# A four-layer decoder step: DVE takes part of the convolution's taps, and attention's queries are split and used ahead of the keys

## What is computed

```python
def conv_module(h, ctx, w_pw1, b_pw1, w_dw, b_dw, ln_g, ln_b, w_pw2, b_pw2):
    a = h @ w_pw1 + b_pw1
    a = a[..., :D_MODEL] * jax.nn.sigmoid(a[..., D_MODEL:])
    full = jnp.concatenate([ctx, a], 1)
    y = lax.conv_general_dilated(full, w_dw[:, None, :], window_strides=(1,), padding='VALID',
                                 dimension_numbers=('NWC', 'WIO', 'NWC'),
                                 feature_group_count=D_MODEL) + b_dw
    y = jax.nn.silu(layer_norm(y, ln_g, ln_b))
    return y @ w_pw2 + b_pw2, full[:, -(CONV_WIDTH - 1):]

def mla_project(h, pos, w_down, g_q, g_kv, w_uq, w_uk):
    ...
    d = h @ w_down
    q_lat = rms_norm(d[..., :MLA_Q_RANK], g_q)                                      # 384
    ckv = rms_norm(d[..., MLA_Q_RANK:MLA_Q_RANK + MLA_KV_RANK], g_kv)               # 256
    kr = rope(d[..., MLA_Q_RANK + MLA_KV_RANK:][:, :, None, :], pos)[:, :, 0]       # 64
    q = (q_lat @ w_uq).reshape(bsz, t, MLA_HEADS, MLA_NOPE + MLA_ROPE)
    ...
```

## Time and profile before

| | us |
|---|---|
| median of 3 runs | 3004.7 |
| lowest and highest | 3002.46, 3007.76 |
| the profiled execution | 3006.55 |
| its span | 3004.8 |
| PE busy in the span | 2908.9 (97%) |
| DVE, POOL, ACT busy | 1643.8 (55%), 1699.8 (57%), 926.0 (31%) |
| convolution, first tap matmul to first statistics product | 864.3 to 989.5 |
| attention, first query transpose to first rope product | 1540.0 to 1553.8 |

### The profile page before, as it was taken

How to read it: one execution, slowest core, us unless ns; L and a number is a source line. 1 busy time by engine, 2 the same in 40 slices (tenths; PEclk the granted TensorE clock), 3 DMA queues, 4 the chain that set the end, 5 groups by cost and what they waited for, 6 DMA issues and landing times.

```text
span 3004.8 us, 53453 instructions
## 1 busy us (share of the span) xinstructions
PE 2908.9 (97%) x21220; PEld 2681.8 (89%) x21220; DVE 1643.8 (55%) x3121; ACT 926.0 (31%) x1813; POOL 1699.8 (57%) x1177
## 2 busy tenths in 40 slices
PE   5999999999999999999989999999999999999997
PEld 4789999999976799999976689999997999999997
DVE  3153684636563784636565548463663536856363
ACT  2220142414230352414233315241423301425141
POOL 2546546868655445857620044685764465468685
PEclk8999999999999999999999999999999999999999
DMA  6643434333344434444321334444422333222332
GB/s 229 249 112 92 124 116 162 99 113 112 100 121 134 170 116 160 151 136 148 97 64 44 95 124 136 148 146 141 140 79 85 96 91 103 67 82 85 88 96 74
DMA packets 450485, 354.84 MB, mean 118 GB/s; under 512 B 26120, under 2 KB 424832, under 8 KB 437933
## 3 DMA queue, kind: packets, MB, share of 16 engines
q1 hardware_dynamic: 435744, 324.79, 35.1%
q10 hardware_dynamic: 14493, 26.63, 3.0%
HBM read 337.86 MB, written 5.25 MB: 114 GB/s over the span
## 4 chain that ended last, share of the span: by engine, by line
PE 81%; DVE 7%; issue 3%; ACT 3%; POOL 2%; DVEq 1%; DMA 1%; POOLq 1%; ACTq 1%; SPq 1%
PE pb L1153 79%; POOL w_lo L1004 1%; DMA ada_first<-in_ada_w 1%; DVE part L2778 1%; ACT h_hi L2145 1%; POOLq L1003 1%; ACT hf L2145 1%; DVE pb L2797 1%; PE pb L1989 1%; DVE xa L2804 0%; DVE h_lo L2828 0%; DVE pr L3107 0%; PE pb L1266 0%; DVE part L2773 0%; ACTq L2442 0%
## 5 line engine op out<-in xcount | busy, mean ns | idle before, releaser
L1001 POOL TENSOR_SCALAR w_hi<-w_raw 128x1024 fp32r<-128x1024 f32 (+2 forms) x272 | 295.9, 1088 | 751.0 <-DMA w_raw<-in_gmlp_w_in 275.7
L1004 POOL TENSOR_TENSOR w_lo<-w_raw,w_hi 128x1024 fp32r<-128x1024 f32 (+2 forms) x272 | 653.1, 2401 | 45.0 <-issue 45.0
L1153 PE MATMUL pb<-a_hi,w_hi 128*128 128x288 f32 x2176 | 593.8, 297 | 2.1 <-DVEq L3392 1.9
L1153 PE MATMUL pb<-a_lo,w_hi 128*128 128x288 f32 x2176 | 588.4, 294 | 0.0
L1153 PE MATMUL pb<-h_hi,w_hi 128*128 128x288 f32 x2144 | 563.9, 299 | 18.0 <-DVE pr L3084 7.9
L1153 PE MATMUL pb<-h_lo,w_hi 128*128 128x288 f32 x2144 | 545.6, 296 | 0.0
L1046 POOL TENSOR_TENSOR w_lo<-w_raw,w_hi 128x512 fp32r<-128x512 f32 x288 | 382.3, 1349 | 180.0 <-DVE s_raw L3049 83.2
L1153 PEld LDWEIGHTS pb<-h_hi,w_hi 128*128 128x128 f32 x2144 | 392.8, 188 | 33.4 <-DVE pr L3084 10.9
L1153 PEld LDWEIGHTS pb<-a_hi,w_hi 128*128 128x128 f32 x2176 | 408.3, 188 | 8.8 <-POOL a_lo L1071 4.2
L1153 PEld LDWEIGHTS pb<-a_lo,w_hi 128*128 128x128 f32 x2176 | 408.6, 188 | 0.8
L1153 PEld LDWEIGHTS pb<-h_lo,w_hi 128*128 128x128 f32 x2144 | 389.5, 189 | 0.0
(11 more groups left out here) (379 smaller groups left out, 4875.9 us busy)
## 6 DMA issues: line engine op xcount, KB each, us to landing
ada_w<-in_ada_w SPq DMA_DIRECT2D x80, 1024.0 KB, 7.7
w_raw<-in_ffn_w_gate SPq DMA_DIRECT2D x88, 512.0 KB, 3.8
w_raw<-in_ffn_w_up SPq DMA_DIRECT2D x88, 512.0 KB, 3.8
w_raw<-in_gmlp_w_in SPq DMA_DIRECT2D x64, 512.0 KB, 4.2
w_raw<-in_ffn_w_down SPq DMA_DIRECT2D x64, 512.0 KB, 4.3
w_raw<-in_gmlp_w_out SPq DMA_DIRECT2D x32, 512.0 KB, 4.7
w_raw<-in_ffn_w_down SPq DMA_DIRECT2D x32, 384.0 KB, 3.9
w_raw<-in_conv_w_pw SPq DMA_DIRECT2D x24, 512.0 KB, 3.9
```

The lines of the kernel that those rows point to most:

```text
L1001: nc.gpsimd.tensor_scalar(w_hi[:, s, 0:w], w_raw[:, s, 0:w], 1.0, 1.0, ALU.mult, ALU.mult).then_inc(split_hi, 1)
L1004: nc.gpsimd.tensor_tensor(w_lo[:, s, 0:w], w_raw[:, s, 0:w], w_hi[:, s, 0:w].bitcast(F32), ALU.subtract).then_inc(split_lo, 1)
L1153: return nc.tensor.matmul(out, lhsT, rhs, start=start, stop=stop)
```

## The change

**Convolution.** `PE_TAPS` gives the groups of taps that stay on PE for each tile: 6, 5, 5, 5, 5, 6, 8, 8. POOL builds only these diagonals. DVE adds the missing 7 (tiles 0 and 5) or 11 taps (tiles 1 to 4) itself, one SCALAR_TENSOR_TENSOR of 512 columns each, from `full` into the bank that PE filled, with a drain behind each, before it takes the bank out. In `taps` the sums of tile m-1 now stand between the two halves of the gate of tile m+2; the rows_ready drain and `complete` follow the second half.

**Attention.** ACT makes the queries' upper parts (`query_upper`), DVE only the lower ones (`query_lower`), as each pair of banks is turned. The queries come first on DVE; scaling and rotating the keys (`scale_keys`, `turn_keys`) and the evacuation of the rope products (`query_rows`) alternate. On PE the rope products stand ahead of the key transposes, which go to the auxiliary banks; ACT copies them after issuing the four output transfers.

```diff
+PE_TAPS = (6, 5, 5, 5, 5, 6, TG, TG)
...
                     last = nc.gpsimd.tensor_tensor(
-                        diag[:, m % 2, q], mask4[:].unsqueeze(1).to_broadcast([P, TG, QC]),
-                        w4[:, q, m, :].unsqueeze(2).to_broadcast([P, TG, QC]), ALU.mult)
+                        diag[:, m % 2, q, 0:PE_TAPS[m]], mask4[:].unsqueeze(1).to_broadcast([P, PE_TAPS[m], QC]),
+                        w4[:, q, m, 0:PE_TAPS[m]].unsqueeze(2).to_broadcast([P, PE_TAPS[m], QC]), ALU.mult)
...
-                    for g in range(TG):
+                    for g in range(PE_TAPS[m]):
                         for q in range(QT):
                             last = mm(out[QC * q:QC * (q + 1), 0:c1 - c0], diag[:, m % 2, q, g, :],
-                                      x4[:, m % 2, q, QT * g + c0:QT * g + c1], g == 0, g == TG - 1)
+                                      x4[:, m % 2, q, QT * g + c0:QT * g + c1], g == 0, g == PE_TAPS[m] - 1)
...
                     if m < KT - 2:
-                        for h in range(2):
-                            gated_in(m + 2, h, h)
-                        dve.drain().then_inc(rows_ready, 1)
-                        complete(m + 2)
+                        gated_in(m + 2, 0, 0)
                     if m:
                         dve.wait_ge(ysq_ready, m)
...
                         last_.then_inc(q_done, 1)
+                    if m < KT - 2:
+                        gated_in(m + 2, 1, 1)
+                        dve.drain().then_inc(rows_ready, 1)
+                        complete(m + 2)
                     sample_taps(m)
-                    v.tensor_scalar(one(yc, m, slice(0, SEQ)), pb[:, aux(), :], one1(par, m, C_DW), None, ALU.add
+                    sums_ = pb[:, aux(), :]
+                    for w in range(QT * PE_TAPS[m], CW):
+                        v.scalar_tensor_tensor(out=sums_, in0=full[:, m % 3, w:w + SEQ], scalar=wdT[:, m, w:w + 1],
+                                               in1=sums_, op0=ALU.mult, op1=ALU.add)
+                        dve.drain()
+                    v.tensor_scalar(one(yc, m, slice(0, SEQ)), sums_, one1(par, m, C_DW), None, ALU.add
                                     ).then_inc(aux_free, 1)
...
+                def query_upper(k):
+
+                    b_p, b_s = [BANKS + (ql_at[0] + 2 * k + i) % BANKS for i in range(2)]
+                    act.wait_ge(ql_turned, 2 * k + 2)
+                    fn(ql_hi[:, k, 0:SEQ], pb[:, b_p, :], ACT.Copy)
+                    fn(ql_hi[:, k, SEQ:], pb[:, b_s, NS:P], ACT.Copy).then_inc(ql_upper, 1)
+
+                for k in range(2):
+                    query_upper(k)
                 square_sums(1, KVR, QR, range(4, TT))
...
+                query_upper(2)
                 act.wait_ge(kv_ready, 1)
...
+                def query_lower(k):
+
+                    dve.wait_ge(ql_upper, k + 1)
+                    for cols, src in ((slice(0, SEQ), slice(0, SEQ)), (slice(SEQ, TOK), slice(NS, P))):
+                        v.tensor_tensor(ql_lo[:, k, cols], pb[:, aux_of(X.n), src], ql_hi[:, k, cols].bitcast(F32),
+                                        ALU.subtract).then_inc(aux_free, 1)
+                        X.up()
...
+                for k in range(3):
+                    query_lower(k)
+                dve.drain().then_inc(lat_ready, 1)
+                scale_keys(2, 0, 4)
+                for n in range(2):
+                    query_rows(n)
+                turn_keys(0, 4)
+                for n in range(2, 5):
+                    query_rows(n)
+                scale_keys(3, 4, TT)
+                turn_keys(4, TT)
                 dve.sem_inc(kv_ready, 1)
-                evac_latents((1, 2))
-                dve.drain().then_inc(lat_ready, 1)
...
+                for n in range(5, 10):
+                    query_rows(n)
+                X.up(BANKS)
```

More of the change, by code:

```diff
@@ L447, in trunk @@
         kt_ready = sem("kt_ready")
-        kt_copied = sem("kt_copied")
+        ql_turned = sem("ql_turned")
+        ql_upper = sem("ql_upper")
         ql_scaled = sem("ql_scaled")
@@ L757, in trunk @@
         turn_at = []
+        ql_at, keys_at = [], []
         stat_banks = {}
@@ L1857, in mla @@
                 pe.wait_ge(ql_scaled, 1)
+                ql_at.append(X.n)
                 for k in range(3):
[L1859 to L1870, removed]
+                    for tts in (range(4), (4,)):
+                        b = aux_bank()
+                        for tt in tts:
+                            last = nc.tensor.transpose(pb[:, b, tt % 4 * P:(tt % 4 + 1) * P],
+                                                       dtok[:, tt, k * P:(k + 1) * P], ident[:])
+                        last.then_inc(ql_turned, 1)
+                        X.up()
                 pe.wait_ge(lat_ready, 1)
@@ L1876, in mla @@
                                   (lambda k: ql_hi[:, k, token_tile(tt)], lambda k: ql_lo[:, k, token_tile(tt)]))
+                pe.wait_ge(kv_ready, 1)
+                pe.wait_ge(aux_free, X.n + BANKS)
+                keys_at.append(X.n)
+                banks = [BANKS + (X.n + i) % BANKS for i in range(BANKS)]
+                for k in range(3):
+                    for tt in range(TT):
+                        rows = (ckv[:, tt, k * P:(k + 1) * P] if k < 2
+                                else kr2[:, tt, :, :].rearrange("p a n -> p (a n)"))
+                        out = pb[:, banks[k], tt * P:(tt + 1) * P] if tt < 4 else pb[:, banks[3], k * P:(k + 1) * P]
+                        last = nc.tensor.transpose(out, rows, ident[:])
+                    last.then_inc(kt_ready, 1)
+                X.up(BANKS)
                 def absorb(h):
@@ L1905, in mla @@
                         absorb(h - 1)
+                    else:
+                        pe.wait_ge(aux_free, X.n + BANKS)
                     expand(aux_bank(), lambda c: ukr[:, c, h * P:(h + 1) * P], lambda c: ckvT[:, c, 0:SEQ])
@@ L2517, in mla @@
                 square_sums(1, KVR, QR, range(4))
-                square_sums(1, KVR, QR, range(4, TT))
[L2519 to L2524, removed]
+                def query_upper(k):
[5 more added lines that the diff above has]
+                    query_upper(k)
+                square_sums(1, KVR, QR, range(4, TT))
+                query_upper(2)
                 act.wait_ge(kv_ready, 1)
@@ L2532, in mla @@
                               ).then_inc(kv_out, 16)
+                key_banks = [BANKS + (keys_at[0] + i) % BANKS for i in range(BANKS)]
+                for k in range(3):
+                    act.wait_ge(kt_ready, k + 1)
+                    fn(ckvT[:, k, 0:SEQ] if k < 2 else krT[:, 0:SEQ], pb[:, key_banks[k], :], ACT.Copy
+                       ).then_inc(aux_free, 1)
+                ps = pb[:, key_banks[3], :]
+                fn(ckvT[:, :, SEQ:], ps[:, 0:2 * P].rearrange("p (k t) -> p k t", k=2)[:, :, NS:], ACT.Copy)
+                fn(krT[:, SEQ:], ps[:, 2 * P + NS:3 * P], ACT.Copy)
+                act.drain().then_inc(aux_free, 1)
                 G.up(10 + 3 * HEADS)
@@ L3456, in scale_queries, with scale_keys @@
                     last_.then_inc(ql_scaled, 1)
-                def latents(n, t0, t1):
+                def scale_keys(n, t0, t1):
                     dve.wait_ge(ssq_ready, n)
@@ L3466, in latents, with turn_keys @@
                                                scalar=ssq[:, tt, 1:2], in1=gqk[:, QR:], op0=ALU.mult, op1=ALU.mult)
+                def turn_keys(t0, t1):
                     cos, sin = rtab[:, t0:t1, 0:half], rtab[:, t0:t1, half:]
@@ L3482, in latents, with query_rows @@
                     dve.drain()
[L3484 to L3487, removed]
+                def query_lower(k):
[3 more added lines that the diff above has]
+                                        ALU.subtract).then_inc(aux_free, 1)
+                        X.up()
+                def query_rows(n):
+                    c, tt = divmod(n, TT)
+                    dve.wait_ge(acc_ready, G.n + 1)
+                    v.tensor_copy(qrt[:, tt, c * 256:(c + 1) * 256], pb[:, G.n % BANKS, 0:256]).then_inc(acc_free, 1)
+                    G.up()
                 for i, (c, tt) in enumerate(first_order(len(DCH))):
@@ L3501, in mla @@
                             scale_queries()
[L3502 to L3505, removed]
-                dve.sem_inc(kv_ready, 1)
-                evac_latents((1, 2))
-                dve.drain().then_inc(lat_ready, 1)
[L3509 to L3514, removed]
+                for k in range(3):
+                    query_lower(k)
[8 more added lines that the diff above has]
+                turn_keys(4, TT)
+                dve.sem_inc(kv_ready, 1)
+                for n in range(5, 10):
+                    query_rows(n)
+                X.up(BANKS)
                 def rotate(tt):
```

## The result

| | before | changed |
|---|---|---|
| median, us (7 runs each, side by side) | 3003.5 | 3015.46 |
| lowest and highest | 3002.34, 3007.76 | 3012.16, 3017.68 |
| ratio | | 1.0037, 95% interval 1.0026 to 1.0049 |
| profiled execution and its span | 3006.55, 3004.8 | 3016.51, 3014.4 |
| statistics of the convolution: first matmul over `yc` starts | 989.48 | 1010.49 |

The account below looks back on a forecast made before the run. PE bounds the kernel before; in the changed convolution DVE, delayed by POOL, was expected to cost more than PE saves. Convolution +14.8 and attention -5.5 gave +9.3 us on 3004.7, so 3014.0 us, range 2992 to 3021.

Parts of the forecast that it names:

- PE's saving, 12.4 us: Convolution: 16 tap groups leave PE, 14.2 us; tile 0's two count nothing, leaving 12.4 us if PE stays the bound.
- The adds, 0.84 us each: Convolution: DVE's 58 added taps take 0.84 us each with drain, 48.7 us together, not held up by POOL.
- Ordinary meetings, 19.4 us: Convolution: DVE instructions wholly in SBUF wait out POOL's where prod_used doesn't set it up; 19.4 us over tiles 0 to 6.
- Built-in meetings, three of four: Convolution, tiles 2 to 5: prod_used releases POOL's 4.1 us product, DVE's bias add waits it out; three times, 12.3 us.
- b: Convolution: DVE's total delay beside POOL, 31.7 us (ends 19.4 and 36); the convolution changes by b - 16.9 us.
- PE waits: Convolution: sign that PE waits on DVE's gate before the products of tiles 5, 6 and 7, four to eight us each.
- Attention, -5.5: Attention: rope products start earlier and key transposes run faster on PE; -5.5 us, ends -7 and -3.
- rival 1: Convolution: DVE wins its meetings with POOL; convolution +2.5, sum -3.0, 3001.7 us; chance 0.21.
- PE stays the bound: Rival for the convolution: DVE's delay at most 4.5 us, the whole 12.4 gained; sum -17.9, 2986.8 us; chance 0.23.
- Rival 3: Convolution: all four built-in meetings are lost and adds take 0.87 us; sum +15.3, 3020.0 us; chance 0.14.

Follow-up runs that it names:

- e10: Changed kernel with tap groups on PE 8, 7, 7, 7, 7, 7, 8, 8 (three DVE adds in tiles 1 to 5); 2995.9 us, 0.9974 of the kernel before.
- e9: Changed kernel with tap groups on PE 6, 6, 6, 6, 6, 6, 8, 8 (seven DVE adds in tiles 0 to 5); 2992.9 us, 0.9966 of the kernel before.
- e7: Changed kernel with tap groups on PE 8, 6, 6, 6, 6, 6, 8, 8 (seven DVE adds in tiles 1 to 5); 2988.3 us, 0.9949 of the kernel before.
- e3: Changed kernel with prod_used given by DVE's 64-column bias add, no longer by the reduce ahead of it; 3001.1 us, 0.9990 of the kernel before.
- e4: Changed kernel with all taps on PE, so no DVE adds; the sums' new place and attention stay; 2997.1 us, 0.9977 of the kernel before.
- e6: Changed kernel with the two sums back behind the copies; adds and attention as changed; 3013.1 us, 1.0029 of the kernel before.
- e2: Changed kernel with all taps on PE and the sums in their old place, so attention's part only; 2996.6 us, 0.9978 of the kernel before.
- e5: Changed kernel with one drain on POOL between its wait for prod_used and its sample product; 3001.0 us, 0.9991 of the kernel before.
- e8: Changed kernel with tap groups on PE 8, 6, 6, 6, 6, 6, 8, 8 and prod_used given by the bias add; 2990.3 us, 0.9958 of before.
- e1: Kernel before with all of the convolution's edits and none of attention's; 3022.1 us, 1.0057 of the kernel before.

## Why the prediction was right, and where only its total was

The number (3014.0; +9.3) came within the interval of what was measured (+7.8 to +14.7), and the direction's reason was the right one. The terms, one by one:

- **PE's saving, 12.4 us.** Right in e10, where one group in five tiles brought 3.2 us of 4.4 with 1.06 more waited before tile 7. I valued tile 0's two groups at nothing; by e9 they cost 2 us, with the clock lower behind the longer wait. The step lacked a price for that. I also wrote that PE's matmuls follow without a gap after the wait before tile 3; the kernel before has 0.72 us before tile 7's taps (984.39). It changed no term of the sum, but it is the wait that grew to 2.21 us in e7.
- **The adds, 0.84 us each.** Eleven take 9.04 us and one 0.75 us, so the step is 0.83. Right, and POOL doesn't hold them up: the earlier trace rows held for a form that also writes into PSUM.
- **Ordinary meetings, 19.4 us.** Adding up what the five SBUF groups of DVE take above their single lengths (0.75, 0.75, 0.28, 0.20, 0.25 us) gives 37.7 us from 872 to 1008. The built-in ones are 16.0 of it, the ordinary ones 21.7. By step, from 0 to 6, the ordinary ones are 4.7, 5.7, 4.5, 2.2, 0, 0.9 and 3.7, where I had 6, 4, 4, 1.4, 0, 0 and 4: laying the two queues beside each other gave nearly the right places too. In e3, without the built-in ones, the sum is 21.0. Tile 0's, the largest single one (4.05), is in e4 as well, which has no adds, and only 1.5 in e6, so it hangs on alignment.
- **Built-in meetings, three of four.** All four happened, 3.97, 4.08, 4.02 and 3.94 us. This is the term that was sized wrong, 12.3 us for 16.0. I let chance decide what a fixed delay decides: POOL's follow-up and DVE's next instruction both hang on the end of the same reduce, so they come the same way each time. With b = 37.7 my own formula gives 37.7 - 16.9 = +20.8 for the convolution; the loop measured +19.9 (864.30 to 989.48 before, 865.39 to 1010.49 now). My forecast had +14.8. With e3's 21.0 it gives +4.1, where +3.1 was measured. The Trainium skill (SBUF — State Buffer, section SBUF: two separate sides) says that of the two instructions that need the shared pair of ports the one that starts first has it for its whole length, and I had worked out +19 with all four lost. That all four were lost agrees with +19 and not with my three. By the records, however, DVE's bias add started 0.04 us before POOL's product and lost; so the recorded starts don't show who gets the ports.
- **PE waits** before tiles 5, 6, 7, 4 to 8 us each: 4.28, 6.37 and 3.04, the last below my range, then 6.21 and 3.70 for tile 5's and tile 6's results, which I hadn't listed.
- **Attention, -5.5.** -5.04 in the changed kernel, -5.44 in e2, where the last wait is shorter. The rope products came 4.7 us after the transposes (I had 5.1), the key transposes took 1.55 us (1.9). At the end PE waited 2.23 us. I had allowed 0 to 2 there, but for the keys; what came late was a rope row that DVE takes out (L3531).

So the convolution was sized 5 us too low, and the total was saved by something that the sum didn't have, which is luck: of the 21.0 us at the statistics only 15.95 were left at the query transposes. 1555.95 against 1540.00 less attention's 5.04 is +10.9. The profile of before has a wait of 2.62 us in the convolution's second stage that the changed kernel doesn't have; of the ten runs e10 alone has it again. PE's timeline of before, of the changed kernel at the same matmuls, and of e10:

```profile
1050.62 0.89 PE L1153 MATMUL pb<-part,ones 128*128 128x288 f32 x2 [2.62 <-DVEq L2779]
```

```profile
1069.85 0.75 PE L1156 MATMUL pb<-part,ones 128*128 128x288 f32 x2
```

```profile
1048.88 0.75 PE L1156 MATMUL pb<-part,ones 128*128 128x288 f32 x2 [2.62 <-DVEq L2806]
```

In before, DVE's L2716 and L2721 take 1.11 and 2.35 us beside POOL's split of weights (a TENSOR_SCALAR at 1033.27, a subtraction at 1034.49). In the changed kernel the same two, L2743 and L2748, take 0.23 and 0.96 us. That is 2.3 us, and the changed kernel's lag behind the kernel before falls from 21.6 us to 19.2 at these matmuls. Most of the rest is PE's clock: before has a lower one behind this wait and again behind a wait of 1.82 us at 1132.64. PE by stretch, before and then the changed kernel at the same work:

```profile
1050.00:1060.00 10.00, 9.38 (x51) 0.83 0.18 52
1130.00:1140.00 10.00, 8.18 (x51) 0.83 0.40 145
```

```profile
1066.00:1076.00 10.00, 9.89 (x63) 1.00 0.21 56
1148.00:1158.00 10.00, 8.16 (x62) 1.00 0.48 166
```

The same matmul over `a_lo` starts at 1054.43 and 1072.02, a lag of 17.6; one over `h_lo` and `s_hi` at 1136.11 and 1152.36, a lag of 16.25. So these two stretches, in part at 1.2 GHz and not 2.4, give back some 1.6 and 1.3 us. e2 has the one at 1132 and another behind a wait of 1.88 us at 1018.91 (0.83 in 1015 to 1025). The changed kernel has the same waits, 1.87 us at 1040.05 and 1.84 at 1150.27, and keeps 1.00. Why the clock falls behind one and not behind the other no run shows. The rivals: 1 and 2 (DVE wins; PE stays the bound) are what e3, e5 and e7 make real, and rival 1's price, 3001.7, is within 1 us of e3's and e5's 3001.1 and 3001.0. Rival 3 had the right count of meetings, 3020.0; it would have been closer in the convolution and 4.5 us too high in all.

## What to carry to other kernels

When a semaphore releases a long POOL instruction in SBUF, look at what the releasing engine does next: if that is a short DVE instruction in SBUF, it may wait out the whole POOL instruction, every time, as here. So give the release one instruction later (e3), or let an instruction with an operand in PSUM come next, as the adds do in e3. When moving work to an engine with slack, fill it to its period less what it already loses to its neighbour, not to its period: 7 adds a tile gained 6 to 9 us (e7 and e8 against e2), 11 lost 17 (e1), with the same code. Work taken from PE ahead of a wait was worth less than nothing here (e9).

## What the runs showed of the hardware that I had not expected

DVE's bias add lost to POOL's product with a recorded lead of 0.04 to 0.05 us, in every one of the four tiles and in e1 and e6 too, and won with one of 0.12 to 0.13 us (e5), also in all four. Tile 0's lost with 0.02 to 0.04 us in the changed kernel, e1, e4 and e5 (4.29 to 4.31 us), beside a product that doesn't wait for the reduce. In the earlier trace rows POOL had been recorded first, by 0.03 to 0.05 us. PE's granted clock can be lower behind a single short idle time: between 870 and 880 it is 1.00 with one of 2.23 us (e7), 0.83 with 2.68 (e1), 2.81 (e5), 3.07 (e6) and 3.43 (e3), 0.66 with 3.35 (e9), but 1.00 with 2.85 in the changed kernel. At 1132.64 of the kernel before 1.82 us were enough, and 1.84 us at the same place of the changed kernel were not. So the length alone doesn't tell it.
